# A decoder step on one core: where TensorE's second count stands in recurrence passes that hold half a mask

## What is computed

```python
score = indexer_scores(qi, wi, ki, valid)        # prompt rows: 1024 keys, sample rows: 8193 keys
_, idx = lax.top_k(score, n_sel)                 # n_sel = 256
k_sel, v_sel = gather_rows(k, idx), gather_rows(v, idx)
o_attn = sparse_attend(q, k_sel, v_sel, valid)

f = lb + (1 - lb) * sigmoid(rf); kk = 1 - f      # recurrence, 1024 tokens, 8 heads
S_t = diag(f_t) S_{t-1} + kk_t i_t^T;  o_t = S_t^T q_t
m = concatenate([o_attn, norm(o_r) * silu(rg)]) @ w_out
```

## Time and profile before

| | us |
|---|---|
| median of 3 runs | 2416.02 (2415.59 to 2416.42) |
| the profiled execution | 2416.54 |
| its span, first to last instruction | 2414.8 |
| mean granted clock of TensorE | 0.990 |

### The profile page before, as it was taken

The page is one execution under the profiler, slowest core; times in us unless marked ns, Lnnn a source line. Parts: engine busy times, 40 slices in busy tenths (PEclk is TensorE's granted clock), DMA queues, the critical chain, the costliest instruction groups (busy, mean ns, idle before and its releaser), DMA issues.

```text
span 2414.8 us, 33393 instructions
## 1 busy us (share of the span) xinstructions
PE 2340.9 (97%) x12317; PEld 1926.6 (80%) x12317; DVE 1612.7 (67%) x2577; ACT 714.9 (30%) x1441; POOL 886.7 (37%) x948
## 2 busy tenths in 40 slices
PE   8999999999999999999999899999999999999996
PEld 7888888888887556778777677888888888888885
DVE  6675666578975348897767844236575665678876
ACT  2122222210023246773332356314122222210014
POOL 5354444446475021110000133414244444445570
PEclk9999999999999999999999999999999999999998
DMA  6021222264411033330010112021012131256401
GB/s 184 18 96 53 88 71 70 100 256 148 144 58 35 1 93 114 105 101 20 2 28 2 41 40 69 4 71 35 27 61 80 62 105 53 73 206 243 144 18 71
DMA packets 138047, 192.58 MB, mean 80 GB/s; under 512 B 19112, under 2 KB 86264, under 8 KB 137632
## 3 DMA queue, kind: packets, MB, share of 16 engines
q1 hardware_dynamic: 130096, 169.97, 21.0%
q0 software_dynamic: 7792, 20.48, 3.0%
HBM read 160.10 MB, written 30.06 MB: 79 GB/s over the span
## 4 chain that ended last, share of the span: by engine, by line
PE 88%; DVE 7%; issue 2%; ACT 1%; POOL 1%; DMA 1%; SPq 0%; DVEq 0%; POOLq 0%; ACTq 0%
PE ps L2104 38%; PE ps L2198 16%; PE ps L794 9%; PE ps L799 7%; PE ps L1186 4%; PE ps L1074 2%; PE ps L2201 2%; PE ps L964 2%; PE ps L1048 2%; PE ps L850 1%; PE ps L875 1%; PE ps L1061 1%; PE ps L1014 1%; PE ps L885 1%; PE ps L897 1%
## 5 line engine op out<-in xcount | busy, mean ns | idle before, releaser
L2104 PE MATMUL ps<-big 128*128 128x258 f32 x1760 | 410.5, 381 | 5.1 <-DVE big L2517 4.6
L2104 PEld LDWEIGHTS ps<-big 128*128 128x128 f32 x1760 | 333.0, 190 | 57.1 <-issue 7.7
L2369 ACT ACTIVATE down_weights<-ps 128x258 f32<-128x258 f32 x370 | 142.8, 387 | 699.8 <-PE ps L2104 699.7
L2637 DVE TENSOR_TENSOR down_weights<-ps,down_weights 128x258 f32<-128x258 f32 x330 | 139.3, 425 | 261.5 <-ACT down_weights L2369 187.1
L794 PE MATMUL ps<-acts,weight_ring 128*128 128x344 f32 x768 | 236.9, 461 | 0.0
L794 PEld LDWEIGHTS ps<-acts,weight_ring 128*128 128x128 f32 x768 | 143.5, 192 | 74.6 <-issue 8.9
L2945 POOL TENSOR_TENSOR big<-weight_ring 128x256 f32<-128x256 f32 x100 | 75.6, 757 | 334.0 <-PE ps L2104 300.1
L2198 PE MATMUL ps<-big,aux 128*128 128x258 f32 x840 | 191.7, 382 | 4.0 <-DVE big L2750 4.0
L2198 PEld LDWEIGHTS ps<-big,aux 128*128 128x128 f32 x840 | 159.8, 191 | 29.6 <-DVE big L2750 5.6
L799 PE MATMUL ps<-weight_ring,acts 128*128 128x256 f32 (+3 forms) x720 | 176.3, 399 | 0.0
L799 PEld LDWEIGHTS ps<-weight_ring,acts 128*128 128x128 f32 (+1 forms) x720 | 126.2, 180 | 37.2 <-issue 9.3
(11 more groups left out here) (456 smaller groups left out, 4464.9 us busy)
## 6 DMA issues: line engine op xcount, KB each, us to landing
big<-scratch_hidden SPq DMA_DIRECT2D x12, 2838.0 KB, 11.0
weight_ring<-ffn_wd SPq DMA_DIRECT2D x8, 2816.0 KB, 9.8
scratch_hidden<-down_weights SPq DMA_DIRECT2D x40, 516.0 KB, 2.8
weight_ring<-ffn_wg SPq DMA_DIRECT2D x20, 1024.0 KB, 7.9
weight_ring<-ffn_wu SPq DMA_DIRECT2D x20, 1024.0 KB, 8.3
down_weights<-ffn_wd SPq DMA_DIRECT2D x4, 2816.0 KB, 20.2
weight_ring<-w_in SPq DMA_DIRECT2D x9, 1024.0 KB, 5.4
big<-x_prompt SPq DMA_DIRECT2D x8, 512.0 KB, 5.5
```

What stands on the lines that cost most here:

```text
L2104: last = M(PS[:, 3 * e + bank, 0:TQ], lhs[:, i, :], rhs[:, i, :], start=begin and i == 0, stop=end and i == n - 1, skip_group_check=True)
L2369: A(st(e, c), PS[:, 3 * e, 0:TQ], ACT.Copy).then_inc(cp_done, 1)
L2637: V.tensor_tensor(out, PS[:, 3 * e + bank, 0:TQ], st(e, part), ALU.add).then_inc(add_done, 1)
```

## The change

In the six passes of `MASK_SLOTS`, TensorE makes all units of the pass, those of `AFTER` too, and only then the count of slot 1. No instruction is added or removed, no other engine's order is changed.

```diff
                     if len(here) > 1:
                         unit(here[0])
-                    if (t, lv, 1) in DEC_SLOTS:
+                    late = (t, lv) in MASK_SLOTS
+                    if (t, lv, 1) in DEC_SLOTS and not late:
                         count(DEC_SLOTS.index((t, lv, 1)))
                     for u in here[1:] if len(here) > 1 else here:
                         unit(u)
...
                         for u in AFTER[t][1:3]:
                             unit(u)
+                    if late and (t, lv, 1) in DEC_SLOTS:
+                        count(DEC_SLOTS.index((t, lv, 1)))
                 pe.wait_ge(h_kt, t + 1)
```

## The result

| | before | after |
|---|---|---|
| median of 9 runs each, taken side by side, us | 2417.62 (2413.17 to 2419.59) | 2424.04 (2416.89 to 2428.36) |
| the profiled execution, us | 2416.54 | 2425.17 |
| its span, us | 2414.8 | 2423.4 |
| mean granted clock | 0.990 | 0.988 |

The ratio is 1.0025, with a 95% interval of 1.0014 to 1.0037: **6.4 us slower**. The prediction was 2422.2 us with a range of 2414.5 to 2427.

The account below looks back on a forecast made before the run. TensorE was taken to bound the kernel (88% of the span). -1.4 us at full clock plus 7.6 for clock falls gave +6.2 on 2416.54, 2422.7; with the median 0.5 lower, 2422.2 us, range 2414.5 to 2427.

Parts of the forecast that it names:

- The price of a meeting: TensorE's moved count to the next count, through DVE's bit and compare: 1.59 us, costing 1.45 to 1.76, taken as 1.6.
- the price's upper end: A meeting costs up to 1.76 us, because a count behind a wait takes 0.59 instead of 0.28.
- Head pair t = 1 at full clock: Passes 3 to 6: four meetings, +6.4, less 5.3 for pass 5's wait, slow count and slow unit: +1.1 us.
- Head pair t = 2 at full clock: Passes 5 and 6: -3.2 at pass 6's level products, +0.7 for the later transposes; -2.5 us in sum.
- The threshold's DMAs: In t = 2 they end some 4 us later within the head pair, covered by some 25 us before their reader.
- The clock: Clock falls behind waits beside level products: four falls of five at 1.9 us, +7.6, on top of -1.4 at full clock.
- the lower bound of my price: A clock fall costs at least 1.7 us, by half of the shortest low stretch, 3.42 us.
- What the prediction said of places: Paired counts end (1,3) to (1,6), the second waiting on DVE's compare; low stretches beside level products at 1197 to 1225.
- That the clock holds: Rival: waits of 1.4 us are too short to matter, leaving -1.4, 2414.6 us; holds or falls once or twice: 0.30.
- Low stretches of 6.83 us throughout: Rival: each of five falls lasts 6.83 us and costs 2.82, 14.1 in all, giving 2428.7 us; chance 0.08.

Follow-up runs that it names:

- the run with filled meetings: The changed kernel plus unread TensorE matmuls between the two counts of each meeting, three, or five in t = 2; ratio 1.0002 to the kernel before, median 2416.93 us.
- the kernel before with filled waits: The kernel before, order unchanged, plus four and seven unread TensorE matmuls in the waits of (1,5) and (2,5); ratio 0.9998, median 2416.86 us.
- the kernel with one unit on either side: The kernel before with units reordered so one stands on each side of the count in (1,5) and (2,5); ratio 0.9961, median 2407.89 us.

## Why the prediction was right

**The price of a meeting** was 1.59 us from count to count and 1.6 in all. Measured: 1.64 from 1198.65 to 1200.29, and 1.96 to the level products. Less the 0.21 that a count had cost ahead of them and the 0.14 at its old place, that is 1.61. (A count behind a wait takes 0.38 at full clock; the 0.59 of the price's upper end was the half clock's.)

**Head pair t = 1 at full clock**: +1.1 was said, the run with filled meetings has +0.80. The wait of 2.14 is gone as said; the slowed unit of 8 rows isn't a counterexample, since the meeting ahead slowed it. The +1.1 is a sum against a kernel that had a fall of its own; with the clock up in both kernels the order costs 3.8, as the kernel before with filled waits shows.

**Head pair t = 2 at full clock**: -2.5 was said. From L1022 of t = 1 the level products of pass 6 start after 1298.13 - 1249.79 = 48.34 us, before after 1292.63 - 1240.98 = 51.65: -3.3, said -3.2 (the wait 2.52, said 2.2). From the level products of pass 7 to the end it takes 1318.81 - 1312.48 = 6.33 us, before 1309.85 - 1303.81 = 6.04: +0.3, where I had said +0.7. The wait of 0.63 for the tails is there (said 0.7), but it took the place of 0.19 us in which the matmuls behind the transposes had waited for ACT. With the 0.14 of pass 6 that makes -3.2, 0.7 better than said. The threshold's DMAs end at 1317.11, 7.2 us later within the head pair where some 4 had been said; their reader starts at 1339.5, so they are covered by 22 us.

**The clock** carried the sign, as said: -1.4 was the forecast without it, and the filled kernel measures no change. But the term was mis-sized. I took four falls of five at 1.9, +7.6. Five of five came, at these prices: 1.69 (5.31 - 3.62, the unit of 8 rows), 1.69 (5.41 - 3.72, the unit of pass 4) and 1.71 (11.21 - 9.50) in t = 1, some 1.2 at its end (1249.79 - 1242.53 = 7.26 from the level products to L1022, filled 6.05), and 3.3 in t = 2 (2.68 - 1.57 and 11.69 - 9.50). Together 9.6. Their mean, 1.92, is the 1.9 that I took; what was left out is the fifth fall. The short stretches cost half of their 3.42 us, as the lower bound of my price had it, and the one of 6.82 us half of that.

So the sum runs 0.8 - 3.2 + 9.6 = +7.2, which is what the stage shows, against +6.2 said; the medians say +6.4. Two errors of opposite sign, 1.0 too little gain at full clock and 2.0 too little loss by the clock, cancel by half. That 6.2 lies so near to the 6.4 of the medians is in part luck: both medians hold low stretches from outside the stage. The time itself came out 1.8 above the 2422.2, of which 1.6 is the kernel before, whose median rose from 2416.02 in three runs to 2417.62 in nine. The Trainium skill, page "TensorE: Matmul & The Clock Gate", section "A second HAM failure mode: psum-queue depth-cycling", tells of a kernel whose short idle times between groups of matmuls were frequent enough for the clock to swing; the five falls behind waits of 1.37 to 2.52 us agree with it. That they must be frequent no run here shows.

**What the prediction said of places** holds for the pairs of counts and for the waits on L1552. Low stretches were told for 1197 to 1225; two came there, two more of t = 1 at 1230 and 1243, and each began on the unit or the transposes behind the level products, or amid them in (2,5).

**The rivals.** That the clock holds is excluded for the profiled execution: all five long meetings were followed by a fall. Its time is what the filled kernel, in which no meeting leaves TensorE idle, comes near to. Low stretches of 6.83 us throughout came once in five; in the run with t = 1 alone one lasted 20.48, so this rival's tail is real.

**What the prediction didn't see** is the second thing that a late count does: it holds DVE too, and through it the mask half and the compare of the next pass. In the full change this stays hidden, since the next count is late as well. Wherever a count is left at its old place behind a moved one it shows: 4.08 us in (1,5), 2.17 in (1,6), 1.70 in (2,6). I missed it again in the expectations for passes 3 and 4 alone and for pass 5 alone. In the kernel before with filled waits I missed its mirror image: there TensorE comes earlier to the next late count, and waits 1.54 us for a DVE that isn't later than before (its compare ends 52.3 us after L1022 of t = 1, before 53.0).

**What stays open**: which executions have low stretches outside the stage (1.74 us of the difference between the profiled executions, the spread of each kernel's runs), and why one stretch lasts 3.42 and another 20.48 us.

## What to carry to other kernels

Where two engines pass a small result back and forth, put independent work on both sides of the hand-over, one piece for each direction; moving the hand-over behind all the work removes the wait on one side and makes a new one at the seam, here six waits for two. Price a wait of TensorE by what its clock does behind it as well as by its length: here five waits that added up to 8 us brought 9.6 us of slower matmuls. A cover taken from one wait is missed at the next one, so follow the waiting engine's own chain for one more pass before a gain is booked.

## What the runs showed of the hardware

- A wait of only 1.37 us was followed by a fall to 1.2 GHz in all four places where it stood ahead of products that use 64 rows, with a stretch of 3.41 to 3.42 us at that level; so it was in two places of two in the kernel with passes 3 and 4 moved, and in four of four in the kernel with t = 1 moved. (In the kernel with pass 5 moved the next wait had begun when the clock fell.) 2.31 us between full-width matmuls had left the clock at 2.4 GHz, and so did 1.54 us ahead of full-width units in the kernel before with filled waits (1.00 from 1291.88 to 1301.56).
- Unread matmuls in the waits (1.54 us of them in a meeting) kept the clock at 1.00 in the whole stage of 120 us of the changed kernel. The fall at the change of head pair, with only 0.44 us of waiting, is another matter: it came in the kernel before with filled waits too (1243.55 to 1246.97), and didn't come in the kernel with one unit on either side, which has no unread matmuls.
- The clock can stay low while TensorE is busy: 20.48 us at 0.50 with 19.82 us busy, amid transposes, matmuls of 64 to 128 columns and the start of a unit.
